# Moving the changed sums into the last pass of the first phase, and the gated sums from VectorE to GpSimd

## The chip, the core and the metric

The program runs on one core of a Trainium2 chip. A core has TensorE (PE in the profile: matmuls, with the weight loads as PEld), VectorE (DVE), ScalarE (ACT), GpSimd (POOL) and SyncE (SP, which here issues most DMAs in order). The metric is the device time of the program in microseconds, the median of repeated runs.

## The reference

One decoder layer with two branches on the same normalised input `h = rmsnorm(x)`, then a gated merge and one output projection:

```
z = h @ w_in                       # split into latents, gates and the pooling input
o = latent attention (MLA)         # per head: o_lat -> w_uv
y_att  = (o * silu(z_att)) @ w_o_att
p      = multi-window causal means of u_pool, minus u_pool, mixed by w_pool
y_pool = (p * silu(z_pool)) @ w_o_pool
merged = sigmoid(g_att) * y_att + sigmoid(g_pool) * y_pool
x      = x + merged @ w_out
y      = rmsnorm(x) * g_final
```

There are 2048 prompt tokens and 8 decoded ones, D_MODEL is 1024, all in float32. Attention and the latents come first; the change concerns what follows them.

## The kernel before

Every float32 product is made of three matmuls on parts: an operand is split into a high part (ScalarE copies it to the type fp32r, `ACT.Copy`) and a low part (VectorE subtracts the high part from the source, `split`, line 93). A weight unit of 128x512 is loaded by SyncE (`load_unit`, line 1338), split high on ScalarE (line 1345) and low on VectorE, and used by TensorE (12 matmuls). Units are numbered by slots; SyncE enters a slot when VectorE has finished the slot's unit, and then loads the unit six slots ahead. ScalarE and VectorE work three slots ahead of TensorE.

What follows the attention has three stages in `merge`:

- **The first phase** multiplies `h` with `w_in`. Four passes (516 tokens each) of 16 groups, 7 units to a group (`SLOTS`). A Strassen-like scheme takes seven products for eight, so it needs sums of quarters of its operands. In each pass GpSimd makes window sums for the pooling branch (`windows`, line 2396, one to four levels, in groups 2 to 5), and in the first three passes also sums of the next pass's `h` (`h_sums`, groups 3, 5, 7, 9). In its last pass, from group 54 on, one latent per group is multiplied with `w_uv` (`value_step`, `values_low`: tiles `d_ols`, `d_gated`, `d_gat`).
- **The second phase** takes five chunks of 412 tokens. A chunk has 24 units: 16 for `w_o_att` (tile `d_gat` moving) and 8 for `w_o_pool` (tile `d_gpl`). VectorE multiplies the results with the gates (`d_saf` with `ya_ok`, `d_spf` with `yp_ok`) and adds both (line 2636, `m_ok`): that is the gated sum, 8 per chunk, stored as `out_mg`. From unit 13 of a chunk on, the next chunk's latents go through `w_uv`: ScalarE copies, GpSimd subtracts (`values_low`, tile `d_ols`), TensorE multiplies.
- **The third phase** (`JOIN`, groups of 256 tokens) multiplies `merged` with `w_out` in the same seven-product scheme, 12 matmuls of 512 columns to a step. Its right operands are `moved` (28 tiles: quarters of `w_out` and sums of quarters), its left ones `kept` (from `staged`, with sums made by GpSimd in `staged_sums`). The order of its first steps is (0,1), (0,2), (0,6), (0,5), (0,7), (1,1), (0,4), (0,3).

The sums of quarters of `w_out` are the changed sums: `change(k)`, k = 0 to 3, each four GpSimd instructions of 128x512 on `quarters` (1 MB, loaded by SyncE), whose result `changed` is stored to `w_moved` (1 MB). One buffer of each is used, so that load k waits for the sums k-1, and sums k wait for store k-1. Before the change, k = 0 and 1 stand in chunk 0 of the second phase, 2 and 3 in chunk 1. In GpSimd's order they stand ahead of the chunk's `values_low`. Of the 28 `moved` tiles, 18 are loaded and split in chunks 2 to 4 (`SPLIT_MOVED`), and the last ten (`raw`) come in at the end of chunk 4: seven are split ahead of or beside the last two gate products, three in step (0,1).

Each engine runs its own list in the order of the code; semaphores (`wait_ge`) connect them.

Of the kernel before, what the change touches and what calls it, by code (L numbers as in the profile page):

```python
# [23 lines left out]
ALU = mybir.AluOpType  # L24
# [46 lines left out]
T = 412  # L71
NC = -(-(SEQ + NDEC) // T)
# [8 lines left out]
HD = KD // 2  # L81
# [1663 lines left out]
UV_AT = 13  # L1745
RAW_ORDER = (21, 22, 23, 18, 19, 20, 24, 25, 26, 27)
GROUPS_C, TAIL_C = 8, 2056 - 2048
# [43 lines left out]
def merge(nc, io, keep, ahead):  # L1791
# [6 lines left out]
    with ExitStack() as ctx:  # L1798
        def at(first, name, shape, dt=f32):
            return nc.alloc_sbuf_tensor_at("d_" + name, shape, dt, offset=first)  # L1800

        def sem(name):
# [61 lines left out]
        moved = [at(first, f"moved{n}", [P, 2, HALF], f32r) for n, first in enumerate(wide_at)]  # L1864
        quarters = at(wide_at[0], "quarters", [P, 4, HALF])
        changed = at(wide_at[2], "changed", [P, 4, HALF])
        moved_f = [at(where["gap"] + n * piece, f"moved_f{n}", [P, HALF]) for n in range(2)]
        raw_at = {m: t_at[0] + (n * piece if n < 3 else 8 * NH * T - (len(RAW_ORDER) - n) * piece)
                  for n, m in enumerate(RAW_ORDER)}
        raw = {m: at(first, f"raw{m}", [P, HALF]) for m, first in raw_at.items()}  # L1870
        assert raw_at[23] + piece <= raw_at[18]
        gfin = at(where["gap"], "gfin", [P, D])
# [112 lines left out]
        STORE_M = {unit_slot(c, 21 + n): (c, n) for c in range(NC) for n in range(KD)}  # L1985
        LOAD_QUARTERS = {unit_slot(k // 2, 3 if k % 2 == 0 else 8): k for k in range(HD)}
        STORE_CHANGED = {unit_slot(k // 2, 7 if k % 2 == 0 else 12): k for k in range(HD)}
        SPLIT_MOVED = {unit_slot(2 + m // 6, 1 + 2 * (m % 6)): m for m in range(12)}
        SPLIT_MOVED |= {unit_slot(NC - 1, 1 + 2 * m): 12 + m for m in range(6)}
        LOAD_MOVED = {s: m for s, m in SPLIT_MOVED.items()}  # L1990
        LOAD_STAGED = {unit_slot(NC - 1, at): i for i, at in enumerate((2, 4, 10, 12))}
        SPLIT_STAGED = {unit_slot(NC - 1, at): i for i, at in enumerate((4, 6, 12, 14))}
        LOAD_RAW = {unit_slot(NC - 1, 19 + k): (2 * k, 2 * k + 1) for k in range(5)}
        SPLIT_RAW = {unit_slot(NC - 1, 21): (21,), unit_slot(NC - 1, 22): (22, 23), UNITS - 1: (18, 19, 20, 24)}
        JOIN_RAW = {(0, 1): (25, 26, 27)}
        JOIN_STAGED = {(0, 1): (0, 1), (0, 2): (2,), (0, 6): (3,)}
        for g in range(1, GROUPS_C - 1):
# [10 lines left out]
        def _(sp):  # L2008
# [67 lines left out]
            for s in range(UNITS):  # L2076
# [75 lines left out]
                if s in LOAD_QUARTERS:  # L2152
                    k = LOAD_QUARTERS[s]
                    sp.wait_ge(unit_ok, FIRST)
# [29 lines left out]
            for n, (g, p) in enumerate(JOIN):  # L2184
# [28 lines left out]
        def _(act):  # L2213
# [111 lines left out]
            for c in range(NC):  # L2325
                for j, (kind, n) in enumerate(TILES_LAST):
                    for a in range(2):
# [46 lines left out]
        def _(pool):  # L2374
# [83 lines left out]
            for g in range(NG_ALL):  # L2458
                if g in H_STEP:
                    h_sums(pool, ahead, H_STEP[g])  # L2460
                if g >= 2 and g - 2 in pool_groups:
                    windows(g - 2)
                if UV_FIRST <= g < UV_FIRST + NH:
                    values_low(0, g - UV_FIRST)
            for c in range(NC):
                for k in range(2 * c, min(2 * c + 2, HD)):
                    change(k)
                if c == NC - 1:
                    for i in range(HD):
                        staged_sums(0, i)  # L2470
                if c < NC - 1:
# [13 lines left out]
        def _(dve):  # L2485
# [131 lines left out]
            for c in range(NC):  # L2617
                for j, (kind, n) in enumerate(TILES_LAST):
                    for a in range(2):
# [71 lines left out]
        def _(pe):  # L2691
# [297 lines left out]
```

## Time and profile before

| | |
|---|---|
| median of 3 runs | 2073.84 us (2071.31 to 2077.46) |
| the profiled execution | 2070.4 us, its span 2068.6 us |
| granted TensorE clock, mean | 0.992 |
| busy: PE, DVE, ACT, POOL | 97%, 72%, 54%, 25% |

The span runs from the first to the last instruction; times in the rows are microseconds from its start. In rows of groups, idle time stands behind the bar with what ended it. The first phase lasts to 1574.6, the second to 1879.5, the third to the end.

### The profile page before, as it was taken

What the parts mean: (1) busy time and instruction counts of PE and PEld (TensorE: products, weight loads), DVE (VectorE), ACT (ScalarE), POOL (GpSimd) and SP (SyncE); (2) the same over time, 40 slices, a digit from 0 to 9 for tenths busy, and PEclk for the clock granted to TensorE, in tenths of its full rate; (3) what the DMA queues carried; (4) which work ended last, traced back from release to release, by engine and by line L of the source; (5) the groups of instructions that cost most, each with busy time, mean ns of one, the idle gap of its engine ahead of it and who ended that gap; (6) DMA issues with size and microseconds to landing.
All of it is one profiled execution on the core that took longest, in us unless ns stands there. A gap on an engine that the chain in (4) does not pass through costs nothing.

```text
span 2068.6 us, 37208 instructions
## 1 busy us (share of the span) xinstructions
PE 2005.8 (97%) x13077; PEld 1831.8 (89%) x13077; DVE 1498.7 (72%) x3208; ACT 1124.5 (54%) x2271; POOL 523.7 (25%) x647
## 2 busy tenths in 40 slices
PE   7999999999999999999999999999999989998998
PEld 6999888888888888699999999999999989997885
DVE  7786887887888776568668758767875777675554
ACT  4446765556555555556665665666564434442442
POOL 3444364333211010213004003101111331122451
PEclk9999999999999999999999999999999999999999
DMA  8876465344221032367776776786888988886452
GB/s 302 267 237 187 121 192 168 112 123 125 90 72 31 6 122 92 129 174 224 245 235 206 248 232 194 259 246 195 252 273 255 322 285 296 289 282 192 135 175 84
DMA packets 284249, 396.97 MB, mean 192 GB/s; under 512 B 34016, under 2 KB 152680, under 8 KB 283032
## 3 DMA queue, kind: packets, MB, share of 16 engines
q1 hardware_dynamic: 278272, 374.26, 58.2%
q0 software_dynamic: 2304, 12.58, 1.6%
q10 hardware_dynamic: 3488, 7.75, 1.2%
q8 instruction: 105, 1.72, 0.3%
q14 instruction: 80, 0.66, 0.1%
HBM read 295.77 MB, written 98.96 MB: 191 GB/s over the span
## 4 chain that ended last, share of the span: by engine, by line
PE 40%; DVE 7%; issue 3%; DMA 3%; ACT 2%; POOL 1%; SPq 1%; ACTq 0%; DVEq 0%; POOLq 0%
PE b_ps L131 40%; DVE d_wr L93 3%; ACT d_wr L1345 1%; DMA d_moved_f<-in_w_quarters 1%; DMA d_quarters<-in_w_quarters 1%; DVE d_pool L93 0%; DVE d_pooled L2594 0%; POOL d_ols L93 0%; DMA d_zsf<-out_zs 0%; DVE d_c L2579 0%; DMA d_olf<-out_olat 0%; DVE d_moved L93 0%; DVE d_gat L93 0%; DVE d_out L2508 0%; DMA d_raw<-in_w_quarters 0%
## 5 line engine op out<-in xcount | busy, mean ns | idle before, releaser
L93 DVE TENSOR_TENSOR d_wr<-d_ws,d_wr 128x512 fp32r<-128x512 f32 x568 | 429.4, 762 | 210.3 <-ACT d_wr L1345 204.2
L1345 ACT ACTIVATE d_wr<-d_ws 128x512 fp32r<-128x512 f32 x568 | 350.1, 628 | 247.7 <-PE b_ps L131 239.5
L131 PE MATMUL b_ps<-d_ht,d_wr 128*128 128x258 f32 x3072 | 398.7, 284 | 6.8 <-DVE d_wr L93 5.2
L131 PEld LDWEIGHTS b_ps<-d_ht,d_wr 128*128 128x128 f32 x3072 | 380.2, 189 | 13.4 <-DVE d_wr L93 12.0
L759 PE MATMUL b_ps<-kt,k_qs 128*128 128x512 f32 (+2 forms) x1520 | 337.8, 370 | 1.2 <-DVE b_p L1147 1.1
L131 PE MATMUL b_ps<-d_hb,d_wr 128*128 128x258 f32 x2304 | 302.7, 284 | 6.2 <-DVE d_wr L93 4.6
L759 PEld LDWEIGHTS b_ps<-kt,k_qs 128*128 128x128 f32 x1520 | 265.4, 188 | 48.5 <-DVE b_p L1147 3.9
L131 PEld LDWEIGHTS b_ps<-d_hb,d_wr 128*128 128x128 f32 x2304 | 287.4, 189 | 9.3 <-DVE d_wr L93 7.3
L1101 ACT ACTIVATE b_pt<-b_ps 128x512 fp32r<-128x512 f32 x272 | 158.3, 597 | 167.5 <-PE b_ps L1207 114.0
L93 DVE TENSOR_TENSOR b_pt<-b_ps,b_pt 128x512 fp32r<-128x512 f32 x272 | 182.9, 688 | 87.8 <-ACT b_pt L1101 86.4
L1207 PE MATMUL b_ps<-b_pt,kv 128*128 128x512 f32 x816 | 227.8, 407 | 0.0
L1094 ACT ACTIVATE b_p<-b_p,b_bias 128x1024 f32<-128x1024 f32 (+7 forms) x192 | 171.6, 896 | 60.0 <-DVE b_low L1154 59.1
L131 PE MATMUL b_ps<-d_gat,d_wr 128*128 128x412 f32 x960 | 184.8, 353 | 2.2 <-DVE d_wr L93 2.2
L131 PEld LDWEIGHTS b_ps<-d_gat,d_wr 128*128 128x128 f32 x960 | 181.7, 191 | 4.0 <-DVE d_wr L93 2.9
L131 PE MATMUL b_ps<-d_moved,d_kept 128*128 128x512 f32 x672 | 160.5, 401 | 7.9 <-DVE d_spf L2630 5.6
L1207 PEld LDWEIGHTS b_ps<-b_pt,kv 128*128 128x128 f32 x816 | 143.4, 189 | 24.2
L131 PEld LDWEIGHTS b_ps<-d_moved,d_kept 128*128 128x128 f32 x672 | 129.1, 192 | 39.1 <-DVE d_spf L2630 5.9
L93 POOL TENSOR_TENSOR k_qs<-k_qf,k_qs 128x512 fp32r<-128x512 f32 (+1 forms) x52 | 71.1, 1368 | 359.8 <-issue 203.2
L1198 PE MATMUL b_ps<-ident,b_p 128*128 128x128 f32 x1088 | 149.0, 273 | 3.3 <-DVE b_pt L93 1.6
L1198 PEld LDWEIGHTS b_ps<-ident,b_p 128*128 128x128 f32 x1088 | 128.4, 140 | 25.6 <-DVE b_pt L93 3.3
L1147 DVE TENSOR_SCALAR_CACHE_REDUCE b_p<-b_ps 128x512 f32<-128x512 f32 (+1 forms) x192 | 125.1, 668 | 14.7 <-PE b_ps L759 13.0
L1171 DVE TENSOR_SCALAR b_p<-b_p,b_inverse 128x1024 f32<-128x1024 f32 (+7 forms) x192 | 133.2, 716 | 0.7
(248 smaller groups left out, 2562.9 us busy)
## 6 DMA issues: line engine op xcount, KB each, us to landing
d_ws<-out_w_sums SPq DMA_DIRECT2D x256, 256.0 KB, 3.5
d_ws<-in_w_pairs SPq DMA_DIRECT2D x192, 256.0 KB, 3.1
d_ws<-in_w_last SPq DMA_DIRECT2D x120, 256.0 KB, 4.4
b_quarters<-in_w_pairs SPq DMA_DIRECT2D x16, 1024.0 KB, 8.1
out_w_sums<-b_sums SPq DMA_DIRECT2D x16, 1024.0 KB, 10.3
out_q<-a_qout SPq DMA_DIRECT2D x32, 384.0 KB, 4.0
d_hf<-out_ht SPq DMA_DIRECT2D x32, 258.0 KB, 3.4
out_zs<-d_out SPq DMA_DIRECT2D x32, 258.0 KB, 4.3
```

The costliest lines, as they stand in the source:

```text
L93: return e.tensor_tensor(low, source, high.bitcast(f32), ALU.subtract)
L131: mm = pe.matmul(out, stationary(a, k), moving(b, k), start=first and k == 0 and a + b == 0, stop=last and k == depth - 1 and a == 1, skip ...
L759: mm = pe.matmul(out, qs[:, a, h, :], keep["kt"][:, first:first + size, b, :], start=k == 0, stop=k == len(pairs) - 1)
L1094: act.activation(span, span, ACT.Exp, bias=bias[:, at:at + 1], scale=-1.0 if negated else SCALE, accum_out=total[:, at, part:part + 1]).th ...
L1101: act.activation(pt[n % NPT][:, 0, :], ps_t[n % NTB][:, :], ACT.Copy).then_inc(pt_hi, 1)
L1147: dve.tensor_scalar(out, inp, 1.0, None, ALU.mult, ALU.max, accum_out=top[:, at, c:c + 1]).then_inc(s_sb, 1)
L1171: dve.tensor_scalar(span, span, inverse[:, at:at + 1], None, ALU.mult).then_inc(p_ok, 1)
L1198: mm = pe.transpose(ps_t[n % NTB][:, h * P:h * P + P], weights(u, h, slice(j * P, j * P + P)), ident[:, :])
L1207: mm = pe.matmul(ps_o[u % 2][:, :], kv[:, j, a, :], pt[n % NPT][:, b, :], start=j == 0 and k == 0, stop=j == tiles(u) - 1 and k == 2)
L1345: act.activation(ahead["wr"][s % WR][:, 0, :, :], ahead["ws"][s % WS][:, :, :], ACT.Copy).then_inc(ahead["w_hi"], 1)
```

## The change

Four things are done. `change(k)` goes to the last pass of the first phase, one in each of the groups 50 to 53 of GpSimd's list, with loads and stores in SyncE's list to match; the buffers lie elsewhere. The gated sum goes from VectorE's list to GpSimd's, behind the `values_low` of three units later. The 18 `moved` tiles are spread over chunks 0 to 4 (4, 4, 4, 4, 2). The ten `raw` tiles are all split in the third phase, in steps (0,1), (0,2) and (0,6), and the splits of `kept` for group 1 move from steps (0,1), (0,2), (0,6) to (0,6), (0,5), (0,7), since those tiles share memory with `raw`; TensorE starts the third phase when the last but one gate product is made, and the last is waited for at step (0,2).

```diff
-RAW_ORDER = (21, 22, 23, 18, 19, 20, 24, 25, 26, 27)
+RAW_ORDER = (18, 19, 20, 21, 22, 23, 24, 25, 26, 27)
...
-        LOAD_QUARTERS = {unit_slot(k // 2, 3 if k % 2 == 0 else 8): k for k in range(HD)}
-        STORE_CHANGED = {unit_slot(k // 2, 7 if k % 2 == 0 else 12): k for k in range(HD)}
-        SPLIT_MOVED = {unit_slot(2 + m // 6, 1 + 2 * (m % 6)): m for m in range(12)}
-        SPLIT_MOVED |= {unit_slot(NC - 1, 1 + 2 * m): 12 + m for m in range(6)}
+        last_pass = PAIRS * (NAP - 1)
+        LOAD_QUARTERS = {SLOT[last_pass + 1, 2] if k == 0 else SLOT[last_pass + 1 + k, 6]: k for k in range(HD)}
+        STORE_CHANGED = {SLOT[last_pass + 2 + k, 6]: k for k in range(HD)}
+        SPLIT_MOVED = {unit_slot(m // 4, (3 if m // 4 else 5) + 3 * (m % 4)): m for m in range(16)}
+        SPLIT_MOVED |= {unit_slot(NC - 1, 7): 16, unit_slot(NC - 1, 9): 17}
...
-        LOAD_STAGED = {unit_slot(NC - 1, at): i for i, at in enumerate((2, 4, 10, 12))}
-        SPLIT_STAGED = {unit_slot(NC - 1, at): i for i, at in enumerate((4, 6, 12, 14))}
+        LOAD_STAGED = {unit_slot(NC - 1, at): i for i, at in enumerate((5, 6, 12, 13))}
+        SPLIT_STAGED = {unit_slot(NC - 1, at): i for i, at in enumerate((9, 10, 14, 16))}
-        SPLIT_RAW = {unit_slot(NC - 1, 21): (21,), unit_slot(NC - 1, 22): (22, 23), UNITS - 1: (18, 19, 20, 24)}
-        JOIN_RAW = {(0, 1): (25, 26, 27)}
-        JOIN_STAGED = {(0, 1): (0, 1), (0, 2): (2,), (0, 6): (3,)}
+        JOIN_RAW = {(0, 1): RAW_ORDER[0:5], (0, 2): RAW_ORDER[5:8], (0, 6): RAW_ORDER[8:10]}
+        JOIN_STAGED = {(0, 6): (0,), (0, 5): (1,), (0, 7): (2, 3)}
...
+            def gated_sum(c, n):
+                pool.wait_ge(yp_ok, c * KD + n + 1)
+                pool.wait_ge(ya_ok, c * KD + n + 1)
+                pool.tensor_tensor(saf[n][:, :], saf[n][:, :], spf[n % 4][:, :], ALU.add).then_inc(m_ok, 1)
...
+                if 0 <= g - 2 - PAIRS * (NAP - 1) < HD:
+                    change(g - 2 - PAIRS * (NAP - 1))
                 if g >= 2 and g - 2 in pool_groups:
                     windows(g - 2)
...
-                for k in range(2 * c, min(2 * c + 2, HD)):
-                    change(k)
...
-                    for h in range(NH):
+                for h in range(KD + 3):
+                    if c < NC - 1 and h < NH:
                         values_low(c + 1, h)
+                    if h >= 3:
+                        gated_sum(c, h - 3)
...
-                        if kind == "OP":
-                            dve.wait_ge(yp_ok, c * KD + out_n + 1)
-                            dve.wait_ge(ya_ok, c * KD + out_n + 1)
-                            dve.tensor_tensor(saf[out_n][:, :], saf[out_n][:, :], gate[:, :], ALU.add).then_inc(m_ok, 1)
...
-            pe.wait_ge(yp_ok, NC * KD)
+            pe.wait_ge(yp_ok, NC * KD - 1)
             pe.wait_ge(ya_ok, NC * KD)
             for g, p in JOIN:
+                if (g, p) == (0, 2):
+                    pe.wait_ge(yp_ok, NC * KD)
```

GpSimd's list in groups 50 and 51 of the last pass, before (window sums of group 48, then of 49; `d_win` are the window buffers):

```order
L2396 TENSOR_TENSOR d_win_13047<-d_u 128x530
L2412 TENSOR_TENSOR d_win_13047<-d_hsum,d_u 128x8
L2396 TENSOR_TENSOR d_win_13047<-d_u 128x530
L2396 TENSOR_TENSOR d_win_13048<-d_win_13047 128x528
L2412 TENSOR_TENSOR d_win_13048<-d_hsum,d_u 128x8
```

and now:

```order
L2434 TENSOR_TENSOR d_changed<-d_quarters 128x512
L2435 TENSOR_TENSOR d_changed<-d_quarters 128x512
L2437 TENSOR_TENSOR d_changed<-d_quarters,d_changed 128x512
L2439 TENSOR_TENSOR d_changed<-d_quarters,d_changed 128x512
L2398 TENSOR_TENSOR d_win_13047<-d_u 128x530
L2414 TENSOR_TENSOR d_win_13047<-d_hsum,d_u 128x8
```

The four changed sums stand ahead of the window sums in each of the four groups; of the second phase the same four rows are gone from two places in chunk 0 and two in chunk 1.

SyncE's list at group 51 of the last pass now (before, the same weight loads follow each other without the two rows in the middle):

```order
L1338 DMA d_ws_12064<-in_w_pairs 128x512
L1338 DMA d_ws_12065<-in_w_pairs 128x512
L1338 DMA d_ws_12066<-in_w_pairs 128x512
L2155 DMA d_quarters<-in_w_quarters 128x4x512
L2160 DMA out_w_moved<-d_changed 128x4x512
L1338 DMA d_ws_12067<-out_w_sums 128x512
```

The load of the next quarters waits there for the four sums before it, and every weight load behind it in the list waits too.

ScalarE's list at the start of the third phase, before, from the last four `raw` tiles on (`d_p1c` and `d_u2c` empty the result banks of steps (0,1), (0,6) and (0,7)):

```order
L2260 ACTIVATE d_moved_13123<-d_raw_13137 128x512
L2348 ACTIVATE d_p1c<-b_ps 128x512
L2260 ACTIVATE d_moved_13124<-d_raw_13138 128x512
L2260 ACTIVATE d_moved_13125<-d_raw_13139 128x512
L2260 ACTIVATE d_moved_13126<-d_raw_13140 128x512
L2270 ACTIVATE d_kept_0_0_13150<-d_staged_13165 128x896
L2270 ACTIVATE d_kept_1_0_13152<-d_staged_13166 128x896
L2270 ACTIVATE d_kept_2_0_13154<-d_staged_13164 128x896
L2352 ACTIVATE d_u2c<-b_ps 128x512
L2270 ACTIVATE d_kept_3_0_13156<-d_staged_13165 128x896
L2355 ACTIVATE d_p1c<-b_ps 128x512
```

and now, from the last two `raw` tiles of step (0,2) on:

```order
L2264 ACTIVATE d_moved_13123<-d_raw_13137 128x512
L2264 ACTIVATE d_moved_13124<-d_raw_13138 128x512
L2354 ACTIVATE d_u2c<-b_ps 128x512
L2264 ACTIVATE d_moved_13125<-d_raw_13139 128x512
L2264 ACTIVATE d_moved_13126<-d_raw_13140 128x512
L2274 ACTIVATE d_kept_0_0_13150<-d_staged_13165 128x896
L2274 ACTIVATE d_kept_1_0_13152<-d_staged_13166 128x896
L2357 ACTIVATE d_p1c<-b_ps 128x512
L2274 ACTIVATE d_kept_2_0_13154<-d_staged_13164 128x896
L2274 ACTIVATE d_kept_3_0_13156<-d_staged_13165 128x896
```

The first `kept` tile of group 1 now stands behind the emptying of step (0,6) (`d_u2c`) and the last two behind that of (0,7).

## Rows read from the trace of the kernel before

**Rows 1.** The page: busy time and share of each engine.

```profile
PE 2005.8 (97%) x13077; PEld 1831.8 (89%) x13077; DVE 1498.7 (72%) x3208; ACT 1124.5 (54%) x2271; POOL 523.7 (25%) x647
```

**Rows 2.** Waits of PE, 1572 to 1912: line, releaser, us in total, times, longest.

```profile
PE b_ps L131 <- POOL d_ols L93: 8.5, 4, 5.5
PE b_ps L131 <- DVE d_spf L2630: 5.6, 1, 5.6
PE b_ps L131 <- DVE d_kept L93: 2.3, 1, 2.3
```

**Rows 3.** Timeline of PE, 1572 to 1912: start, length, operands, count, idle before.

```profile
1574.57 33.96 PE L131 MATMUL b_ps<-d_gat,d_wr 128*128 128x412 f32 x180
...
1636.52 33.95 PE L131 MATMUL b_ps<-d_gat,d_wr 128*128 128x412 f32 x180
...
1702.51 15.93 PE L131 MATMUL b_ps<-d_gat,d_wr 128*128 128x412 f32 x84
...
1762.14 34.03 PE L131 MATMUL b_ps<-d_gat,d_wr 128*128 128x412 f32 x180
...
1821.70 15.93 PE L131 MATMUL b_ps<-d_gat,d_wr 128*128 128x412 f32 x84
...
1885.24 16.77 PE L131 MATMUL b_ps<-d_moved,d_kept 128*128 128x512 f32 x60 [5.58 <-DVE d_spf L2630]
```

**Rows 4.** Stretches behind two waits: us, busy per engine, PEclk, DMA share, GB/s.

```profile
1885.00:1891.00 6.00, 5.76 (x14) 4.50 (x15) 3.18 (x6) 0.23 (x1) 1.37 (x4) 0.50 0.54 133
...
1904.30:1908.50 4.20, 4.20 (x11) 3.32 (x12) 2.20 (x3) 0.60 (x1) 4.04 (x8) 0.59 0.60 184
```

**Rows 5.** Timeline of POOL, chunk 0.

```profile
1603.06 1.30 POOL L2426 TENSOR_TENSOR d_changed<-d_quarters 128x512 f32<-128x512 f32 x1 [9.75 <-DMA d_quarters<-in_w_quarters]
...
1608.96 2.53 POOL L93 TENSOR_TENSOR d_ols<-d_olf,d_ols 128x412 fp32r<-128x412 f32 x2
```

**Rows 6.** Timeline of ACT, chunk 4.

```profile
1837.47 0.63 ACT L2255 ACTIVATE d_moved<-d_moved_f 128x512 fp32r<-128x512 f32 x1 [5.92 <-DMA d_moved_f<-out_w_moved]
```

**Rows 7.** Timeline of ACT, end of chunk 4.

```profile
1881.02 3.75 ACT L2260 ACTIVATE d_moved<-d_raw 128x512 fp32r<-128x512 f32 x7 [7.47 <-DMA d_raw<-in_w_quarters]
```

**Rows 8.** The last staged tile of group 1: timelines of SP, POOL, DVE.

```profile
1896.75 0.33 SPq L2049 DMA_DIRECT2D d_staged<-out_mg  x1
```

```profile
1900.23 0.46 POOL L2439 TENSOR_TENSOR d_staged<-d_staged 128x128 f32<-128x128 f32 x1 [3.30 <-DMA d_staged<-out_mg]
```

```profile
1903.15 1.09 DVE L93 TENSOR_TENSOR d_kept<-d_staged,d_kept 128x896 fp32r<-128x896 f32 x1 [3.68 <-ACT d_kept L2270]
```

**Rows 9.** Groups 37, 50 and 53 of the first phase, columns as in rows 4.

```profile
1278.80:1292.50 13.70, 11.91 (x91) 11.10 (x91) 12.60 (x18) 7.58 (x17) 8.97 (x8) 1.00 0.57 166
...
1416.90:1427.00 10.10, 10.10 (x86) 10.10 (x86) 7.09 (x13) 5.71 (x12) 0.82 (x2) 1.00 0.64 187
...
1449.20:1460.90 11.70, 11.09 (x91) 10.87 (x91) 10.15 (x17) 6.66 (x15) 5.75 (x5) 1.00 0.66 203
```

**Rows 10.** Timelines of DVE, beside window sums and without them.

```profile
1431.86 2.98 DVE L93 TENSOR_TENSOR d_wr<-d_ws,d_wr 128x512 fp32r<-128x512 f32 x2
```

```profile
1436.65 0.68 DVE L93 TENSOR_TENSOR d_wr<-d_ws,d_wr 128x512 fp32r<-128x512 f32 x1
```

**Rows 11.** Timeline of SP, chunk 0: a load of quarters.

```profile
1596.58 0.44 SPq L2156 DMA_DIRECT2D d_quarters<-in_w_quarters  x1
```

**Rows 12.** Weights in group 53: SP's issue, ACT's use, median us to landing.

```profile
1444.31 5.14 SPq L1338 DMA_DIRECT2D d_ws<-out_w_sums  x4
```

```profile
1451.44 0.62 ACT L1345 ACTIVATE d_wr<-d_ws 128x512 fp32r<-128x512 f32 x1
```

```profile
d_ws<-in_w_pairs SPq DMA_DIRECT2D x10, 256.0 KB, 3.1
```

**Rows 13.** Timeline of POOL, end of chunk 3.

```profile
1806.58 1.09 POOL L93 TENSOR_TENSOR d_ols<-d_olf,d_ols 128x412 fp32r<-128x412 f32 x1 [1.39 <-ACT d_ols L2246]
```

**Rows 14.** POOL's second changed sum: ns min/median/max.

```profile
L2427 POOL TENSOR_TENSOR d_changed<-d_quarters x4: 1283/1291/2935, 1588.6 to 1669.8; 128x512 f32<-128x512 f32 x4
```

More of the change, by code:

```diff
@@ L1864, in merge @@
         moved = [at(first, f"moved{n}", [P, 2, HALF], f32r) for n, first in enumerate(wide_at)]
-        quarters = at(wide_at[0], "quarters", [P, 4, HALF])
-        changed = at(wide_at[2], "changed", [P, 4, HALF])
+        quarters = at(t_at[0], "quarters", [P, 4, HALF])
+        changed = at(t_at[0] + 16 * HALF, "changed", [P, 4, HALF])
         moved_f = [at(where["gap"] + n * piece, f"moved_f{n}", [P, HALF]) for n in range(2)]
-        raw_at = {m: t_at[0] + (n * piece if n < 3 else 8 * NH * T - (len(RAW_ORDER) - n) * piece)
-                  for n, m in enumerate(RAW_ORDER)}
+        raw_at = {m: t_at[0] + n * piece for n, m in enumerate(RAW_ORDER)}
         raw = {m: at(first, f"raw{m}", [P, HALF]) for m, first in raw_at.items()}
-        assert raw_at[23] + piece <= raw_at[18]
+        assert len(RAW_ORDER) * piece <= 8 * NH * T
         gfin = at(where["gap"], "gfin", [P, D])
@@ L2153, in _ @@
                     k = LOAD_QUARTERS[s]
-                    sp.wait_ge(unit_ok, FIRST)
+                    sp.wait_ge(unit_ok, SLOT[last_pass - 1, 3] + 1)
                     wait(sp, t_ok, added_t + 4 * k if k else 0)
@@ L2165, in _ @@
                         sp.wait_ge(changed_out, H_BASE + 16 * HD)
+                        sp.wait_ge(sig_ok, len(sig_count))
+                        sp.wait_ge(unit_ok, FIRST)
                     load_moved(LOAD_MOVED[s])
@@ L2189, in _ @@
                     load_x(g + 1)
-                if (g, p) == (0, 6):
+                if (g, p) == (1, 1):
+                    sp.wait_ge(added, add_join[0, 5])
                     load_x(1)
@@ L2248, in value_step @@
                     h = step - 2
+                    if c == 0 and h == 0:
+                        act.wait_ge(changed_out, H_BASE + 16 * HD)
                     act.wait_ge(gated_ok, c * NH + h + 1)
@@ L2340, in _ @@
                             high_staged(0, SPLIT_STAGED[s])
-                        for m in SPLIT_RAW.get(s, ()):
-                            high_raw(m)
             for n, (g, p) in enumerate(JOIN):
@@ L2470, in _ @@
                         staged_sums(0, i)
-                if c < NC - 1:
-                    for h in range(NH):
+                for h in range(KD + 3):
+                    if c < NC - 1 and h < NH:
                         values_low(c + 1, h)
+                    if h >= 3:
+                        gated_sum(c, h - 3)
             pool.memset(half_c[:, :], -0.5).then_inc(win_step, 1)
@@ L2645, in _ @@
                             low_staged(0, SPLIT_STAGED[s])
-                        for m in SPLIT_RAW.get(s, ()):
-                            low_raw(m)
             for n, (g, p) in enumerate(JOIN):
@@ L2781, in _ @@
                 if g == 0:
-                    pe.wait_ge(moved_ok, MOVED_OK + {5: HD * MOVED_OF[5] + HD, 7: 18 + 5}.get(p, HD * MOVED_OF[p] + HD))
+                    pe.wait_ge(moved_ok, MOVED_OK + HD * MOVED_OF[p] + HD)
                 if p == 1:
```

## The prediction

> **What bounds the kernel now.** I read the page first: TensorE is busy for 97% of the span [rows 1], so a change is worth what it takes from TensorE's waits, and costs what it adds to them. Next I read TensorE's waits from the end of the first phase into the third [rows 2]. There are three kinds: 8.5 us for `d_ols` from GpSimd (four times, 5.5 at most), 5.6 us for the last gate product (`d_spf`), 2.3 us for `d_kept`. The timeline shows where [rows 3]: the chunks start at 1574.57, 1636.52, 1702.51, 1762.14 and 1821.70, the third phase at 1885.24 after 5.58 of idle time, so chunk 4 ended at 1879.66. The chunks take 61.95, 65.99, 59.63, 59.56 and 57.96 us. Chunks 0 and 1, which hold the changed sums, are the long ones. Chunk 4 has no value products; at 33.96 us for 15 units [rows 3] its 24 units would take 54.3, so 3.6 are lost there. Last, the windows behind two waits [rows 4]: after the idle 5.58 the granted clock is 0.50 (1.2 GHz in place of 2.4) for 6 us, which costs another 3.0; behind the wait of 2.3 it is 0.59 over 4.2 us, which costs 1.7. So a wait there is paid nearly twice.
>
> **Chunks 0 and 1: the changed sums leave.** In GpSimd's list the sums stand ahead of `values_low`. One set takes 5.9 us (1603.06 to 1608.96), and its load holds GpSimd before that for 9.75 [rows 5]. When they are done, two overdue `d_ols` run at once; that is the 8.5 us of [rows 2]. Without them chunks 0 and 1 have nothing that chunks 2 and 3 lack, so I take those as their length: 61.95 and 65.99 become 59.6 each, **-8.7** (bounds -8.0 and -9.4, by half a microsecond or less per chunk for other `moved` tiles).
>
> **Chunk 4.** ScalarE waits 5.92 us there for a `moved` tile from DMA [rows 6], and the weight copies queue behind it; TensorE's lost 3.6 us are this. Now only two `moved` tiles are left in the chunk, at units 7 and 9 in place of six, and the staged loads start later. I take 0.5 us as left: **-3.1** (bounds -3.6 and 0).
>
> **The seam.** Before, ScalarE waits 7.47 us for `raw` tiles [rows 7], VectorE stands behind it with the gate products still to make, and TensorE waits 5.58. Now the raw tiles come after step (0,1), and the third phase starts when chunk 4 ends; the last product and sum take about 0.6 and 1.1 to 1.5 us on VectorE and GpSimd, inside the first step. A step at full clock takes (16.77 - 3.0) / 5 = 2.75 us [rows 3, 4]. What is late next is `kept` of group 1, wanted at step (1,1), 13.8 us after the start. Its first tile is split only behind step (0,6), at 8.3, then the emptying of a bank and two raw copies (3.75 / 7 = 0.54 each [rows 7], 1.6 in all), then copy and split (about 1.0 and 1.09 [rows 8]): 12.0. SyncE's load of the last staged tile waits for that buffer. From its issue at 1896.75 to the end of the split at 1904.24 it is 7.5 us [rows 8], so (1,1) starts near 20 rather than 13.8. TensorE waits about 6 us, and as behind the like wait of before, I add 3.0 for the clock. Before: 24.6 us from the end of chunk 4 to the start of (1,1), plus 1.7 of clock, 26.3. Now: 20.2 + 3.0 = 23.2. **-3.1** (bounds -6 with a faster load and little lost clock, -1 with a slower one). The later load of `x` for group 1 has some five steps (14 us) before it is wanted; I cost it at nothing. Uncovered it would cost its landing, some 5 us.
>
> **The last pass.** Sixteen GpSimd instructions, 4 x 5.9 = 23.6 us, now lie in groups 50 to 53. Two things can hurt.
>
> First VectorE. A weight split takes 0.68 us alone, and 2.98 / 2 = 1.49 beside window sums [rows 10]. VectorE is busy 7.09 of 10.1 us in group 50 and 10.15 of 11.7 in group 53, with 0.82 and 5.75 us of GpSimd work [rows 9]. Group 37, with the same window sums and `h` sums beside them, has 8.97 us and takes 13.70 [rows 9]: 3.2 us more on GpSimd lengthen the group by 2.0, part of which is VectorE's own work on `h`. I take 0.5 us for group 50, where VectorE has 3 us of room, and 1.5 to 2 each for groups 51 to 53: +6.
>
> The Trainium skill ("SBUF — State Buffer", section "Who interferes with whom") says that a VectorE instruction with two SBUF inputs contends with a GpSimd instruction that reads SBUF, and that the loser of the shared pair blocks fully. The 1.49 of [rows 10] agrees with it. If all 23.6 us locked VectorE out, beyond its room (3.0 us in group 50, 1.55 in group 53, so some 9 over the four), this would be +15 in place of +6; it is the first rival.
>
> Second, SyncE. The load of quarters k and the store of k-1 stand in its list between weight loads and wait for the four sums before. A load takes 6.5 us from issue to use (1596.58 to 1603.06 [rows 5, 11]), so a round is 12.4 or longer, against 10.1 to 11.7 for a group. SyncE is held some 2 us longer at each round, up to 7 at the last store. A weight load of group 53 is issued at 1444.31, used at 1451.44 and lands in 3.1 [rows 12]: 4 us of cover. Without cover each microsecond would be TensorE's. Groups stretched by VectorE give the rounds room, so I count it inside the 6 us. **+6** for the pass (bounds +2, if VectorE's room takes it, and +15).
>
> **The gated sums.** VectorE loses 40 instructions, off TensorE's path, and I cost that at nothing: the room it gives lies in chunks where TensorE is the limit. GpSimd gains 40 of the shape of `d_ols`, 1.09 us at best [rows 13], and their place matters: a sum stands between two `values_low`, 20 times in the chunks with values. GpSimd is idle for 1.39 us before the split [rows 13], so a sum of 1.1 to 1.4 just fits; below nothing I exclude, since VectorE isn't waited for. **+1** (bounds 0, and 1.5 x 20 = 30 if each ran as long as the slowest changed sum, 2.94 [rows 14]).
>
> **Sum:** -8.7 - 3.1 - 3.1 + 6 + 1 = -7.9 us. It is made against the profiled execution (2070.4 us, span 2068.6), which would come to 2062.5; that execution lies 3.4 under the median of 2073.84, so the median comes to 2065.9.
>
> **The rivals.**
>
> *The last pass eats the gain.* By the mechanism of [rows 10], with the pass at +12 to +15 and the wait at (1,1) at 8 us rather than 6, the sum is -1 to +3: 2073 to 2077, no change. For it speaks group 37 with 13.70 us [rows 9]; against it, that VectorE's sums from PSUM go on beside GpSimd, and that group 37 has VectorE work of its own.
>
> *GpSimd's list comes late (slower).* Its place is units 16 to 20 of chunks 0 to 3: a gated sum that is still running delays the next `d_ols`, and TensorE waits as in [rows 2]. The room is 1.39 us. At 2.94 us a sum the 20 places cost up to 30 us, net +21. It decides from a mean of about 2.1 us a sum: 0.7 x 20 = 14, net +6, 2080. For it speaks the slowest changed sum of 2.94 [rows 14]; against it the 1.29 median there.
>
> *The pass hides it.* With +2 in the last pass and the early bounds at the seam the sum is -13 to -15: 2060. For it: VectorE's 3 us of room in group 50. Against it: only 1.55 in group 53.
>
> **How the numbers follow.** The forecast 0.50, the pass eats it 0.30, GpSimd late 0.09, hidden 0.11. 0.3% is 6.2 us, about what a measurement can tell from no change. Of the forecast's 0.50 I give 0.03 to a gain under that, so faster 0.47 + 0.11 = 0.58, same 0.30 + 0.03 = 0.33, slower 0.09. Forecast and hidden alone span 2058 to 2068.5; with most of the case that eats the gain the range goes to 2074.5. It leaves out the slower case and the rest of the no-change case.
>
> **What would show it.** `d_ols` should be gone from TensorE's waits in chunks 0 and 1, both at 59 to 60 us. No wait at the third phase's start, but one of 5 to 7 us for `d_kept` at (1,1), with the clock at half behind it. Groups 50 to 53, from 44.0 us now (1416.9 to 1460.9), should take 48 to 52, weight splits beside `d_changed` at 1.3 us or more. The gated sums on GpSimd should last 1.1 to 1.5. It is wrong if groups 50 to 53 take over 55 us, if `d_ols` comes back as a wait in all chunks, or if the wait at (1,1) is over 9 us.

## The result and the profile after

The changed kernel takes 2080.12 us in the median, against 2073.84 before: a ratio of 1.0039, with a 95% interval of 1.0029 to 1.0049. It is slower, where the prediction said 2065.9 and faster. The profiled execution has a span of 2076.2 us, 7.6 more than before.

TensorE's waits from the last pass into the third phase, then its timeline at the chunks' starts, the third phase's start and step (1,1) (to compare with [rows 2, 3]):

```profile
PE b_ps L131 <- DVE d_wr L93: 15.6, 13, 2.7
PE b_ps L131 <- DVE d_kept L93: 8.8, 1, 8.8
PE b_ps L131 <- DVE d_gat L93: 1.3, 4, 0.3
PE b_ps L131 <- DVE d_spf L2640: 1.1, 4, 0.3
PE b_ps L131 <- POOL d_ols L93: 1.0, 2, 0.6
```

```profile
1591.39 33.96 PE L131 MATMUL b_ps<-d_gat,d_wr 128*128 128x412 f32 x180
...
1651.30 2.41 PE L131 MATMUL b_ps<-d_gat,d_wr 128*128 128x412 f32 x12
...
1711.68 2.41 PE L131 MATMUL b_ps<-d_gat,d_wr 128*128 128x412 f32 x12
...
1772.78 2.41 PE L131 MATMUL b_ps<-d_gat,d_wr 128*128 128x412 f32 x12
...
1833.70 2.41 PE L131 MATMUL b_ps<-d_gat,d_wr 128*128 128x412 f32 x12
```

```profile
1888.39 14.09 PE L131 MATMUL b_ps<-d_moved,d_kept 128*128 128x512 f32 x60
1911.23 18.96 PE L131 MATMUL b_ps<-d_moved,d_kept 128*128 128x512 f32 x71 [8.75 <-DVE d_kept L93]
```

Read as differences of starts, the span divides without a remainder:

| stretch | before | after | difference | predicted |
|---|---|---|---|---|
| to the end of the first phase | 1574.57 | 1591.39 | +16.8 | +6 |
| chunks 0 and 1 | 127.94 | 120.29 | -7.6 | -8.7 |
| chunks 2 and 3 | 119.19 | 122.02 | +2.8 | +1 (all gated sums) |
| chunk 4 | 57.96 | 54.69 | -3.3 | -3.1 |
| end of chunk 4 to (1,1) | 24.64 | 22.84 | -1.8 | -3.1 with the next line |
| (1,1) to the end | 164.3 | 165.0 | +0.7 | |

The gains in chunks 0, 1 and 4 came nearly as worked out. The seam gave about a third of its term, and chunks 2 and 3 lost more than was allowed for all gated sums. The loss in the last pass is almost three times its term, and all of it lies in groups 50 to 53. Their windows (columns as in [rows 4]):

```profile
1416.90:1428.20 11.30, 10.42 (x87) 10.21 (x86) 8.55 (x13) 5.72 (x12) 6.69 (x5) 1.00 0.72 208
1428.20:1443.90 15.70, 12.31 (x87) 11.41 (x85) 10.84 (x14) 7.26 (x15) 9.42 (x7) 0.89 0.71 238
1443.90:1460.60 16.70, 11.86 (x90) 11.04 (x90) 12.35 (x17) 6.71 (x14) 10.79 (x8) 1.00 0.73 246
1460.60:1477.70 17.10, 11.89 (x90) 11.06 (x90) 13.52 (x17) 6.47 (x13) 12.50 (x9) 1.00 0.87 308
```

They take 60.8 us in place of 44.0; the stretch from group 54 to the end of the phase is as long as before. In none of them is VectorE (third busy column) busy all the time. The four groups as one window, then a part of group 51:

```profile
1416.90:1477.70 60.80, 46.49 (x350) 43.73 (x348) 45.26 (x58) 26.16 (x53) 39.40 (x29) 0.97 0.76 254
...
1434.90:1437.90 3.00, 2.95 (x12) 2.65 (x12) 3.00 (x3) 1.79 (x4) 2.92 (x3) 0.51 0.42 121
```

Before, TensorE was busy 42.72 of the 44.00 us. So 13.0 of the 16.8 us are waits, and 3.8 are matmuls that take longer. A part of the 3.8 is the clock: behind a wait of 2.26 us the granted clock is 0.51 (the lower level, 1.2 GHz) from 1434.9 on, and 12 matmuls take 2.95 us where they take 1.60 at full clock.

SyncE's waits from 1405 to 1478, then the loads' landing in the four groups (median us at the end of a row), after and then before:

```profile
SPq L1338 <- DVE d_wr L93: 38.7, 27, 5.0
SPq L99 <- POOL d_changed L2439: 8.4, 2, 4.2
SPq L2160 <- POOL d_changed L2439: 4.2, 1, 4.2
```

```profile
out_w_moved<-d_changed SPq DMA_DIRECT2D x4, 1024.0 KB, 8.9
d_ws<-out_w_sums SPq DMA_DIRECT2D x16, 256.0 KB, 8.7
d_ws<-in_w_pairs SPq DMA_DIRECT2D x12, 256.0 KB, 5.4
```

```profile
d_ws<-out_w_sums SPq DMA_DIRECT2D x16, 256.0 KB, 2.8
d_ws<-in_w_pairs SPq DMA_DIRECT2D x12, 256.0 KB, 2.9
```

SyncE stands 12.6 us for the changed sums, and the weight loads that it then issues land in 5.4 to 8.7 us where they took 2.8 to 2.9. GpSimd itself waits for the store before it:

```profile
1433.03 1.26 POOL L2434 TENSOR_TENSOR d_changed<-d_quarters 128x512 f32<-128x512 f32 x1 [9.29 <-DMA out_w_moved<-d_changed]
...
1448.94 1.27 POOL L2434 TENSOR_TENSOR d_changed<-d_quarters 128x512 f32<-128x512 f32 x1 [6.25 <-DMA out_w_moved<-d_changed]
```

A round (from one set of sums to the next) is 15.9 us, not 12.4. So two things are at work, VectorE's slower instructions and the transfers, and the trace alone doesn't divide the 16.8 us between them.

### The profile page after: what moved, and what is told of

It reads as the page before. It is cut to its first block, busy times and chain, and to the rows that moved or that the text cites. A ratio compares the mean times of both kernels' runs of the same rounds, so it can differ in the third digit from the quotient of the medians.

```text
span 2076.2 us, 37210 instructions
## 1 busy us (share of the span) xinstructions
PE 2004.8 (97%) x13077; PEld 1825.7 (88%) x13077; DVE 1507.7 (73%) x3168; ACT 1127.5 (54%) x2271; POOL 586.1 (28%) x687
## 4 chain that ended last, share of the span: by engine, by line
PE 37%; DVE 9%; DMA 4%; issue 3%; ACT 2%; POOL 1%; SPq 1%; ACTq 0%; DVEq 0%; POOLq 0%
PE b_ps L131 37%; DVE d_wr L93 3%; DVE d_gat L93 2%; ACT d_wr L1345 1%; DMA d_zsf<-out_zs 1%; DMA out_w_moved<-d_changed 1%; DVE d_spf L2640 1%; DMA d_spf<-out_sp 1%; DMA d_moved_f<-out_w_moved 1%; DMA d_moved_f<-in_w_quarters 0%; DVE d_pool L93 0%; DMA d_ws<-out_w_sums 0%; DVE d_moved L93 0%; DVE d_pooled L2604 0%; DVE d_c L2589 0%
```

## The experiments

All are edits of the changed kernel, and the diffs are shortened (`...` stands for lines left out). Ratios are to the kernel before, run again beside each of them (medians of 2071.2 to 2072.0), with a 95% interval; the changed kernel stands at 1.0039. Lengths of groups and chunks are read from one profiled execution of each kernel.

**The last pass: the sums without the transfers (sums_only).**

```diff
-LOAD_QUARTERS = {SLOT[last_pass + 1, 2] if k == 0 else SLOT[last_pass + 1 + k, 6]: k for k in range(HD)}
+LOAD_QUARTERS = {SLOT[last_pass + 1, 2]: 0}
-STORE_CHANGED = {SLOT[last_pass + 2 + k, 6]: k for k in range(HD)}
+STORE_CHANGED = {SLOT[last_pass + 6, 6]: 0, SLOT[last_pass + 7, 2]: 1, SLOT[last_pass + 7, 5]: 2, SLOT[last_pass + 8, 1]: 3}
...
```

> The changed kernel with one load of quarters in place of four (so that all four sets of sums are made of the first quarters, which leaves out three quarters of the changed sums' result) and the four stores moved behind group 54; the sixteen sums on GpSimd stay in groups 50 to 53. Theory A, the transfers: the loads and stores of 1 MB each and SyncE's waits for the sums hold the weight loads back; without them groups 50 to 53 take 45 to 49 us (44.0 before the change, 60.8 with it). Theory B, the shared port: the 23.6 us of sums beside VectorE do it; groups 50 to 53 still take 55 to 61 us. My prediction put this part at +6, thus 50.

Groups 50 to 53 took 53.6 us: between the theories, with more than half of the loss still there. The four groups as one window, first of the kernel before, then of this run, and VectorE's weight splits in each (line, shapes, count, busy us, mean ns):

```profile
1416.90:1460.90 44.00, 42.72 (x350) 42.09 (x349) 35.31 (x58) 24.90 (x53) 13.96 (x14) 1.00 0.60 180
```

```profile
1417.00:1470.60 53.60, 45.54 (x350) 43.88 (x348) 46.32 (x58) 25.20 (x53) 38.91 (x30) 0.97 0.51 153
```

```profile
L93 DVE TENSOR_TENSOR d_wr<-d_ws,d_wr 128x512 fp32r<-128x512 f32 x28 | 24.4, 877 | 8.9 <-ACT d_wr L1345 8.9
```

```profile
L93 DVE TENSOR_TENSOR d_wr<-d_ws,d_wr 128x512 fp32r<-128x512 f32 x28 | 30.1, 1096 | 7.9 <-ACT d_wr L1345 7.9
```

The same 58 instructions of VectorE take 11.0 us more beside 25.0 us more of GpSimd, while the DMA share is lower than before. All of TensorE's waits there are for `d_wr` (8.1 us, 6.8 more than before); the other 2.8 of the 9.6 us are again matmuls that take longer. VectorE is still idle for 7.3 of the 53.6 us, so its free time is not what TensorE had as cover. That is the lead of a single split: in group 50 of the kernel before the splits end 0.3 to 1.3 us ahead of their first matmul. The split with the shortest lead, before, then the same split in this run and TensorE behind it:

```profile
1420.20 0.69 DVE L93 TENSOR_TENSOR d_wr<-d_ws,d_wr 128x512 fp32r<-128x512 f32 x1 [1.10 <-ACT d_wr L1345]
```

```profile
1420.80 1.62 DVE L93 TENSOR_TENSOR d_wr<-d_ws,d_wr 128x512 fp32r<-128x512 f32 x1 [1.10 <-ACT d_wr L1345]
```

```profile
1422.48 3.19 PE L131 MATMUL b_ps<-d_ht,d_wr 128*128 128x258 f32 x24 [0.96 <-DVE d_wr L93]
```

The split takes 0.93 us longer, and TensorE waits 0.96.

**The transfers without most of the sums (short_sums).**

```diff
+                width = 8 if k else HALF
-                pool.tensor_tensor(to[:, 0, :], of[:, 1, :], of[:, 0, :], ALU.subtract).then_inc(t_ok, 1)
+                pool.tensor_tensor(to[:, 0, 0:width], of[:, 1, 0:width], of[:, 0, 0:width], ALU.subtract).then_inc(t_ok, 1)
...
```

> The changed kernel with the changed sums of sets 1 to 3 cut from 512 to 8 columns (which leaves out most of them); all loads, stores and waits as they are. Theory A, the transfers: the loads and stores still go out in pairs ahead of weight loads, only the round is shorter by some 6 us; groups 50 to 53 take 50 to 56 us. Theory B, the shared port: with three of four sets gone the loss goes with them; 45 to 48 us.

Groups 50 to 53 took 50.9 us, as theory A has it:

```profile
1417.40:1468.30 50.90, 45.63 (x350) 43.77 (x349) 38.32 (x59) 25.73 (x53) 21.21 (x29) 0.97 0.89 303
```

SyncE never waits for a sum here (its waits from 1405 to 1478 are all for units), and still the weights land late:

```profile
SPq L1338 <- DVE d_wr L93: 48.7, 38, 4.6
```

```profile
d_ws<-out_w_sums SPq DMA_DIRECT2D x16, 256.0 KB, 7.3
```

So transfers of 1 MB that are issued in a pair just ahead of weight loads cost by themselves: the four groups lose 6.9 us, of which 1.9 lie in group 50 with the one full set of sums, which leaves some 5 (an estimate). Sums 9.6 and transfers 5 make 14.6 of the 16.8. The rest appears only with both; SyncE's 12.6 us of waiting for sums do so too, but no run shows that they are the rest. The whole program of this run stands at 0.9984 (0.9974 to 0.9994).

**Sums in every other group (spread).**

```diff
-LOAD_QUARTERS = {SLOT[last_pass + 1, 2] if k == 0 else SLOT[last_pass + 1 + k, 6]: k for k in range(HD)}
-STORE_CHANGED = {SLOT[last_pass + 2 + k, 6]: k for k in range(HD)}
+CHANGE_AT = {last_pass + 2 + 2 * k: k for k in range(HD)}
+LOAD_QUARTERS = {SLOT[last_pass + 1 + 2 * k, 2]: k for k in range(HD)}
+STORE_CHANGED = {SLOT[last_pass + 2 + 2 * k, 7]: k for k in range(HD)}
...
```

> The changed kernel with the four sets of sums in every other group (50, 52, 54, 56), each load of quarters 14 to 15 slots after the one before, and each store two slots ahead of the next load; the buffers lie where nothing is written before group 58. The sums are all made. Theory A, the transfers: with a round of some 21 us SyncE waits for no sums and never sends two transfers at once; groups 50 to 56 lose 2 to 5 us to the kernel before instead of 16.8, and the median is 2066 to 2069. Theory B, the shared port: the same 23.6 us of sums lie beside VectorE, two sets of them in groups with window sums; the pass loses at least 8, the median is 2072 to 2076.

The pass lost 12.0 us (its end at 1586.58 against 1574.57), the ratio is 1.0000 (0.9991 to 1.0009). Without SyncE's waits for sums and without pairs the loss falls by 4.8, not more, as theory B has it. The loads and stores of 1 MB are still there, one at a time, so this run doesn't say how much of the 12.0 is the sums alone. A piece of it took another way, as the window sums behind a changed sum came late and with them the pooling product:

```profile
1586.58 33.96 PE L131 MATMUL b_ps<-d_gat,d_wr 128*128 128x412 f32 x180
```

```profile
1489.83 0.80 PE L131 MATMUL b_ps<-d_ols,d_wuv 128*128 128x412 f32 x3 [2.63 <-DVE d_gpo L2619]
```

**Sums in the second phase again, in GpSimd's free stretches (chunks).**

```diff
-LOAD_QUARTERS = {SLOT[last_pass + 1, 2] if k == 0 else SLOT[last_pass + 1 + k, 6]: k for k in range(HD)}
-STORE_CHANGED = {SLOT[last_pass + 2 + k, 6]: k for k in range(HD)}
+LOAD_QUARTERS = {unit_slot(k // 2 + k % 2, 4 if k % 2 else 21): k for k in range(HD)}
+STORE_CHANGED = {unit_slot(k // 2 + 1, 10 if k % 2 else 3): k for k in range(HD)}
...
```

> The changed kernel with the changed sums back in the second phase, but in stretches where GpSimd has nothing else: sets 0 and 1 at the start of chunk 1, sets 2 and 3 at the start of chunk 2, each done before unit 13, where the values begin; the buffers lie in the home of four moved tiles that come in later. Theory G: where VectorE has room at every unit and no d_ols stands behind the sums, they cost nothing: the first phase ends near 1574.6 as before the change, chunks 1 and 2 take 60.4 to 61.2 as in the changed kernel, and the median is 15 to 17.5 us under the changed kernel's. Rival H: the transfers of 1 MB beside the weight loads, or the slower splits, hold TensorE there too; chunks 1 and 2 take 63 us or more, and the median is 8 to 12 under the changed kernel's.

Theory G fell. The last pass was as before the change, but chunks 1 and 2 took 71.4 and 66.1 us; the ratio is 1.0033 (1.0021 to 1.0045). ScalarE in chunk 1:

```profile
1651.18 0.63 ACT L2257 ACTIVATE d_moved<-d_moved_f 128x512 fp32r<-128x512 f32 x1 [6.82 <-DMA d_moved_f<-in_w_quarters]
1651.71 1.13 ACT L1345 ACTIVATE d_wr<-d_ws 128x512 fp32r<-128x512 f32 x2
```

The load of a `moved` tile stands behind a transfer of 1 MB, ScalarE waits 6.82 us for it, and two weight copies wait behind ScalarE. TensorE loses 2.75 us there, and later in the chunk it waits 4.02 us for `d_ols`.

**Sums back at their old place (sums_back).**

```diff
+LOAD_QUARTERS = {unit_slot(k // 2, 3 if k % 2 == 0 else 8): k for k in range(HD)}
+STORE_CHANGED = {unit_slot(k // 2, 7 if k % 2 == 0 else 12): k for k in range(HD)}
...
```

> The changed kernel with the changed sums alone put back where they were before (loads at units 3 and 8 of chunks 0 and 1, stores at 7 and 12, sums ahead of the chunk's values); the eight moved tiles that now come in beside them in chunks 0 and 1 stay. Theory J: the last pass's 16.8 us go, and chunks 0 and 1 get back the 8 us that the sums cost before: together 126 to 130 us, with d_ols as a wait again; the median is 7 to 10 under the changed kernel's. Rival H: beside the moved tiles and the other loads of these chunks the transfers hold the weights back, as they did at the start of chunks 1 and 2; chunks 0 and 1 take 133 us or more together, and the median is within 4 of the changed kernel's.

Rival H, and beyond its bound: chunks 0 and 1 took 69.2 and 75.2 us, the ratio is 1.0065 (1.0052 to 1.0079), the slowest of all. The same queue on ScalarE, and what TensorE makes of it:

```profile
1604.27 0.63 ACT L2258 ACTIVATE d_moved<-d_moved_f 128x512 fp32r<-128x512 f32 x1 [8.58 <-DMA d_moved_f<-in_w_quarters]
1604.80 1.65 ACT L1345 ACTIVATE d_wr<-d_ws 128x512 fp32r<-128x512 f32 x3
```

```profile
1608.44 9.37 PE L131 MATMUL b_ps<-d_gat,d_wr 128*128 128x412 f32 x36 [6.67 <-DVE d_wr L93]
```

So the parts of the change hang together: with `moved` tiles in chunks 0 and 1 the changed sums can't stay there. The pair best2 and best3 below, which differ in this alone, shows the same.

**Gated sums back on VectorE (gated_back).**

```diff
...
-                    if h >= 3:
-                        gated_sum(c, h - 3)
...
+                        if kind == "OP":
+                            dve.wait_ge(yp_ok, c * KD + out_n + 1)
+                            dve.wait_ge(ya_ok, c * KD + out_n + 1)
+                            dve.tensor_tensor(saf[out_n][:, :], saf[out_n][:, :], gate[:, :], ALU.add).then_inc(m_ok, 1)
```

> The changed kernel with the gated sums back on VectorE, at the place that they had before. Theory E: on GpSimd they cost TensorE about 1.2 us in each of chunks 1 to 3 (60.39, 61.10 and 60.92 us in place of 59.6), through d_ols and through two small waits at every chunk's end (for d_spf and d_gat, 0.3 each) that the kernel before does not have; back on VectorE the chunks take 59.5 to 59.8 and the median falls by 3 to 4. Rival F: the moved tiles, now spread over all chunks, do it; the chunks stay at 60.4 to 61.1 and the median within 1 us of the changed kernel's.

The ratio is 1.0019 (1.0008 to 1.0029). The small waits for `d_spf` and `d_gat` at the chunks' ends are gone; chunks 0 to 3 take 59.1, 60.2, 60.0 and 61.0 us, 240.3 in all, which is 2.05 less, and chunk 4 takes 0.6 less. That is more than executions differ: in the seven kernels that share the second phase of the changed kernel (that one, sums_only, short_sums, spread and the three of the seam) chunks 0 to 3 take 241.7 to 243.2. TensorE's waits in chunks 0 to 3 now:

```profile
PE b_ps L131 <- POOL d_ols L93: 2.2, 3, 1.0
PE b_ps L131 <- DVE d_wr L93: 1.2, 3, 0.8
```

Theory E is right on the chunk ends and wrong on `d_ols`, which stays without the sums. So the gated sums cost some 2.6 us in these two executions; chunk 3 is at 61.0 for another reason, which was not followed. What the gated sums do on GpSimd shows in VectorE's splits of `d_gat` (the values), from 1574 to 1834, first in the changed kernel, then in this run:

```profile
L93 DVE TENSOR_TENSOR d_gat<-d_gated,d_gat 128x412 fp32r<-128x412 f32 x33 | 44.8, 1358 | 1.1 <-ACT d_gat L2254 1.1
```

```profile
L93 DVE TENSOR_TENSOR d_gat<-d_gated,d_gat 128x412 fp32r<-128x412 f32 x33 | 21.1, 640 | 1.1 <-ACT d_gat L2254 1.1
```

Beside the gated sums the same 33 splits take 23.7 us more, and the 30 gated sums of this stretch take VectorE 20.9 us in this run. So the move took nothing off VectorE in chunks 0 to 3, by the same means as in the last pass.

**The seam, three steps (raw_ahead, seam, seam2).** The first moves five raw splits ahead:

```diff
-JOIN_RAW = {(0, 1): RAW_ORDER[0:5], (0, 2): RAW_ORDER[5:8], (0, 6): RAW_ORDER[8:10]}
+JOIN_RAW = {(0, 1): RAW_ORDER[5:8], (0, 2): RAW_ORDER[8:10]}
...
+            for m in RAW_ORDER[0:5]:
+                high_raw(m)
...
+            for m in RAW_ORDER[0:5]:
+                low_raw(m)
```

The loops stand ahead of the third phase's steps in ScalarE's and in VectorE's list.

> The changed kernel with the first five raw tiles copied and split before the emptying of step (0,1), in place of behind it, the next three behind (0,1) and the last two behind (0,2). Theory C: the wait of 8.75 us for kept at step (1,1) comes of VectorE's row of ten splits, which starts at 1892.76 only, 4.4 us after the third phase; three microseconds earlier there, the wait is 5 to 6.5 us and the median 2076 to 2078. Rival D: it comes of GpSimd's sums of staged tiles and their loads; the wait stays 8 to 9 us and the median within 1 us of the changed kernel's.

The second also loads staged tiles early (`load_staged(1, 0)`, `load_staged(1, 2)` ahead of the last `store_m`) and splits kept 0 in (0,2):

> The changed kernel with the raw tiles split as in the run before it (five ahead of the emptying of step (0,1), three behind it, two behind (0,2)), and with the staged tiles 0 and 2 of group 1 loaded ahead of the last stores of the second phase rather than behind them, so that kept 0 can be split behind step (0,2) and free its buffer for the load of tile 3. Theory D: what is left of the wait at step (1,1) is the late load of the staged tiles and the load of tile 3 behind it; the wait falls from 8.75 us (7.17 with the raw tiles alone) to 0 to 2 us, with less of half clock behind it, and the median by 7 to 10. Rival I: GpSimd's sums of the staged tiles, which VectorE's splits slow, are the bound; the wait stays at 4 to 6 us and the median falls by 3 to 5.

The third loads tile 0 alone early and splits kept 0 behind the first five raw tiles:

> The changed kernel with the raw tiles split as in the run raw_ahead, with staged tile 0 of group 1 alone loaded ahead of the last stores, and kept 0 made directly behind the first five raw splits, whose memory alone it takes. Theory I: the four tiles of kept are a chain through GpSimd's sums (2.7 us each beside VectorE's splits) and the one buffer that tile 3 shares with tile 0; with tile 0 some 4 us earlier and no store held up, the wait at step (1,1) falls to 3 to 5 us (8.75 in the changed kernel, 7.17 and 6.29 in the two runs before), the median by 4 to 6. Rival: the chain hangs on the load of tiles 1 and 2 behind the stores; the wait stays at 6 to 7.

The wait at (1,1), in this order:

```profile
1907.53 22.66 PE L131 MATMUL b_ps<-d_moved,d_kept 128*128 128x512 f32 x88 [7.17 <-DVE d_kept L93]
```

```profile
1909.60 20.66 PE L131 MATMUL b_ps<-d_moved,d_kept 128*128 128x512 f32 x80 [6.29 <-DVE d_kept L93]
```

```profile
1910.84 14.38 PE L131 MATMUL b_ps<-d_moved,d_kept 128*128 128x512 f32 x52 [5.20 <-DVE d_kept L93]
```

The ratios are 1.0029 (1.0018 to 1.0040), 1.0027 (1.0017 to 1.0038) and 1.0023 (1.0013 to 1.0034). No single link was the bound. Theory C's splits gave 1.6 us of the 8.75, less than its 2.3 to 3.8. In the second run the stores stood behind the early loads and the load of tile 1 behind the stores; theory D missed by 4 us, and its rival's 4 to 6 is nearer. The third, at 5.2, is just over theory I's 3 to 5.

**Together (best2, best3).** Both have the sums of sums_back, the gated sums of gated_back and the seam of seam2. The second takes the `moved` tiles out of chunks 0 and 1:

```diff
-SPLIT_MOVED = {unit_slot(m // 4, (3 if m // 4 else 5) + 3 * (m % 4)): m for m in range(16)}
-SPLIT_MOVED |= {unit_slot(NC - 1, 7): 16, unit_slot(NC - 1, 9): 17}
+SPLIT_MOVED = {unit_slot(2 + m // 7, 1 + 2 * (m % 7)): m for m in range(14)}
+SPLIT_MOVED |= {unit_slot(NC - 1, 1 + 3 * m): 14 + m for m in range(4)}
```

> Changed sums at the old place, gated sums on VectorE, and the seam of the run beside it, all in one. By the sum of the three, -8 -3 -5 to the changed kernel: 2062 to 2066, 6 to 10 under the kernel before. If the chunks 0 and 1 with moved tiles beside the sums are late (rival H), 2068 or more.

> The same as the run before it, but the 18 moved tiles come in with 7, 7 and 4 to chunks 2 to 4, none beside the changed sums. By rival H chunks 0 and 1 take 126 to 128 us together, as in the kernel before, and the median is 2061 to 2066; if the moved tiles beside the sums cost nothing, it stands within 1 us of the run before it.

The run best2 stands at 1.0029 (1.0018 to 1.0041), by rival H. The run best3 is faster than the kernel before: 2066.80 us against 2071.21 beside it, 0.9977 (0.9968 to 0.9986), just over the 2066 that was expected at most. An earlier one (best), with the changed sums of chunks, the gated sums on VectorE and the first loads of seam, stood at 1.0021 (1.0012 to 1.0030), over all that was expected of it: chunk 1 alone was 73.8 us there.

> The three edits of the other runs of this call together: the changed sums in GpSimd's free stretches of chunks 1 and 2, the gated sums on VectorE, and the early loads and splits at the seam. If the costs add up as theories D, E and G have it, the median is 25 to 30 us under the changed kernel's and 17 to 23 under that of the kernel before (2050 to 2055); if one of them comes back elsewhere, as a wait for d_ols in chunk 1 or 2 or as a new one behind step (1,1), 2056 to 2065.

In best3 chunks 0 and 1 are 61.6 and 68.4 us, 130.0 together where best2 has 141.5 and 126 to 128 were expected. It is ahead of the kernel before at the seam, 19.6 us from the end of chunk 4 to (1,1) where that has 24.6, and in chunk 4 (56.4 for 58.0). What is left is the wait of before, longer:

```profile
PE b_ps L131 <- POOL d_ols L93: 10.8, 5, 7.8
PE b_ps L131 <- DVE d_kept L93: 5.5, 1, 5.5
```

## Why the prediction was wrong

**The last pass** is the step that failed. It had two parts.

First VectorE: "I take 0.5 us for group 50, where VectorE has 3 us of room, and 1.5 to 2 each for groups 51 to 53". Group 50 lost 1.2 us and group 53 5.4. The price of a split beside GpSimd [rows 10] was about right, and the room [rows 9] was the wrong cover. TensorE uses a split every 1.45 us, and in group 50 each has a lead of 0.3 to 1.3 us; a split that is late by 0.9 can be a wait, even where VectorE is idle a microsecond later. Sums alone cost 9.6, matmuls at the lower clock among them; the prediction priced the clock at the seam and put it at nothing in the pass.

The Trainium skill ("SBUF — State Buffer", section "Who interferes with whom") has the loser of the shared pair fully blocked for an instruction. Here VectorE lost 11.0 us to 25.0 us of GpSimd (sums_only). So VectorE locked out for the whole time of the sums, from which the prediction has +15, is too much, and +15 came near the 16.8 by luck: a part of those is the transfers.

Second SyncE: "a round is 12.4 or longer", and "I count it inside the 6 us". A load alone took 6.5 us [rows 5, 11], but load k and store k-1 are let go by the same sums and leave together, and the store lands in 8.9 (median); the round was 15.9. And the term counted only how long SyncE stands, not what its next loads find ahead of them: 5.4 to 8.7 us to landing in place of the 3.1 of [rows 12], against 4 us of cover.

**The rivals.** The first had the place and half of the mechanism, VectorE beside GpSimd, with the pass at +12 to +15 and a wait of 8 at (1,1); the transfers were not in it, and at 16.8 and 8.75 the sum went past "no change". The second, GpSimd late, names 2080, which is the time that came, but not by its mechanism: a gated sum took 1.45 us in the mean, not 2.1, and TensorE waited 1.0 us in all for `d_ols`. The sign that the prediction named for itself, over 55 us in groups 50 to 53, came. By their own terms the first rival's sum starts at 0, not -1, and the second's nets +5, not +6; neither changes the forecast.

**Chunks 0 and 1, chunk 4:** right in mechanism, and nearly in size: -7.6, just outside the bounds of -8.0 and -9.4, and -3.3. `d_ols` is gone as a wait in chunks 0 and 1, with 1.0 us left in chunks 2 and 3. In the reading of [rows 2] a fourth kind of wait is missing, for `d_wr`, 2.2 us in chunks 2 and 4.

**The seam:** -1.1 for -3.1. No wait at the start, as foretold; at (1,1) 8.75 in place of 6. The step was "the emptying of a bank and two raw copies (...), then copy and split: 12.0". It counted ScalarE's copies, where VectorE's ten raw splits were the longer row, and the copy of `kept` stood behind the last of them:

```profile
1892.76 3.37 DVE L93 TENSOR_TENSOR d_moved<-d_raw,d_moved 128x512 fp32r<-128x512 f32 x5 [3.59 <-ACT d_moved L2264]
...
1896.65 4.25 DVE L93 TENSOR_TENSOR d_moved<-d_raw,d_moved 128x512 fp32r<-128x512 f32 x5
1901.93 1.09 DVE L93 TENSOR_TENSOR d_kept<-d_staged,d_kept 128x896 fp32r<-128x896 f32 x1 [1.02 <-ACT d_kept L2274]
```

They end at 1900.90, 12.5 us after the start, and the first split of `kept` at 1903.02, 14.6 after it, not 12.0. From the issue of the last staged load at 1903.16 to the end of its split the 7.5 us of the prediction were 8.0. The run raw_ahead shows that the raw splits are a part of the wait (1.6 us), not the whole. The half clock behind the wait came (0.58 over 6 us):

```profile
1911.20:1917.20 6.00, 5.97 (x16) 4.73 (x17) 0.00 (x0) 0.60 (x1) 3.73 (x9) 0.58 0.70 219
```

**The gated sums** last as long as foretold:

```profile
L2425 POOL TENSOR_TENSOR d_saf<-d_saf,d_spf 128x412 f32<-128x412 f32 x40 | 57.9, 1448 | 29.1 <-DVE d_spf L2640 29.1
```

Their cost is some 2.6 us, not 1, and not where it was sought: with them on GpSimd TensorE waits twice for 0.3 us at each chunk's end, for VectorE's results. The prediction costed what VectorE loses at nothing, since it got rid of 40 instructions; its splits of `d_gat` beside the sums took 23.7 us more.

## What to carry to other kernels

An engine's idle share is no cover for its late instructions: take the lead of each result on its use, and compare that with the delay of one instruction. Work that goes from VectorE to GpSimd is weighed with what it adds to VectorE's instructions beside it. A large transfer is priced by what is issued behind it on the same queue and by who stands in order behind those loads, not by its own landing. A move of one piece is tried together with the pieces that gave room for it: of the places tried, the changed sums were cheapest where they had been, as long as no `moved` tiles were loaded beside them.

## What the hardware showed

- Weight loads of 256 KB from `out_w_sums`, issued behind pairs of 1 MB transfers, landed in 7.3 to 8.7 us (median; runs short_sums and after), against 2.8 before; 1 MB stores landed in 8.9 where a load of 1 MB leaves with them, and in 5.3 in best3, where they don't leave together.
- In sums_only 25 us of two-input sums on GpSimd made VectorE's instructions 11 us longer, nearly all of it in those with two SBUF inputs; the sums and products of 128x258 with a PSUM input took 0.41 to 0.42 us as before.
- A VectorE split of 128x412 took 1.36 us in the mean beside the gated sums on GpSimd, and 0.64 with them on VectorE (gated_back).
